# Reordering the end of the values stage of a fused decoder layer: own values before the last pages, two banks for norm sums, sample columns before variances and branch rounding

## The chip, the cores and the metric

The kernel runs on one core of one Trainium2 chip. The metric is the device time of one execution in microseconds (us), start to end, with the weights, the paged cache and the inputs in HBM. Of the kernel before there are three timed runs: 783.63, 785.12 and 786.19 us, median 785.12 us.

## The reference, cut to what matters

One inference step of a hybrid decoder layer for 256 prompt tokens and 8 sample sequences (one new token each, 1024 past tokens in pages of 128), D_MODEL 1024, all in float32:

```python
h = rms_norm(x) * (1.0 + sc2) + sh2
proj = h @ lp["w_in"]                  # q, k, v of both branches, gates g_a, g_b
o_a, o_b = attend(q_a, k_a, v_a, q_b, k_b, v_b, lam)
o_b = rms_norm(o_b, lp["subln_diff"]) * (1.0 - lam_init)
y_a = o_a.reshape(B, T, WIDTH_A) @ lp["w_branch_moba"]
y_b = o_b.reshape(B, T, WIDTH_B) @ lp["w_branch_diff"]
mixed = (jax.nn.sigmoid(g_a) * y_a + jax.nn.sigmoid(g_b) * y_b) @ lp["w_out"]
x = x + g2 * mixed
```

Before it and behind it stands a gated feed-forward block (D_FF 2816). `attend` is block-sparse attention (branch A, 8 heads of 64) and differential attention (branch B, 4 heads with values of 128); sample tokens read past keys and values through a page table. The lines above are the stretch that the change touches: the last of `attend`, the norm of `o_b`, and the two branch products.

## The kernel before, in words

Activations lie transposed: 128 features on the partitions, 264 columns (256 prompt tokens, then the 8 sample tokens) along the free axis. There are eight feature chunks c of 128; chunks 0 to 3 are branch A, 4 to 7 branch B. Every float32 weight product is made of three matmuls of rounded parts: ScalarE makes the high part of a weight block (`hi`, tile whi, line 671), VectorE or GpSimd the rest (`lo`, tile wlo, line 969 on VectorE, line 626 on GpSimd), and TensorE multiplies high by high, high by low and low by high (lines 1433 to 1435). Weight blocks have numbers; W_BR to W_BR + 3 are the four halves of the two branch matrices, W_OUT follows. whi and wlo have two buffers each, taken in turn.

The order of the work is written out by hand, engine by engine; semaphores join the engines, and each engine runs its own list strictly in that order. In the **values stage** TensorE goes through c = 0 to 7. For each c it multiplies two halves of a sequence's value pages with padded weights (line 1789, tiles kvA and kvB, three slots each, `_lent` is the third), for c = 3 and c = 7 adds the new tokens' own values (line 1803, `dcur` by `vtoks`), turns the prompt probabilities (line 1815), sums squares of a chunk of branch B over the partitions (`o_sum`, line 1772, bank 7), multiplies the prompt values (lines 1837 and 1838), and for c = 3 and c = 7 extracts the sample outputs from the masked accumulators (line 1845, 16 records of 4 columns). VectorE masks those accumulators (`om`, line 1340), takes each sum to a reciprocal variance (`o_variance`, lines 1305 and 1306), makes the low part of the branch A output (`hlo`, line 1353) and copies the extracted sample columns into qT (line 1356). ScalarE rounds these sample columns (line 925), squares those of branch B (line 926), then takes the sigmoid of all gates (line 929, after a table load), then the square root of the reciprocal variances (line 693, after another table load). VectorE scales the branch B output by it (line 1367), ScalarE rounds it (line 932), VectorE takes its low part (line 1370).

The **branch products** are four: q = 0, 1 with branch A's output into banks 0 to 3 and 4 to 7, then q = 2, 3 with branch B's output into the same banks. Each is 48 matmuls. q = 2 waits for branch B's low part (`s_olo`), for its weights, and for `s_turned_g`: VectorE must have multiplied q = 0's result by the gates (line 1378) before its banks are written again. On VectorE that instruction stands behind the low part of branch B (line 1370) and the two halves of `lo(W_BR + 2)` (line 969).

GpSimd issues the DMAs of branch B's pages in this stage (line 443), then four loads of the last conditioning weights (last_ada, line 643). SyncE issues branch A's pages and all weight blocks; a weight block's load waits until `lo` of the block that held its slot is done.

Of the kernel before, what the change touches and what calls it, by code (L numbers as in the profile page):

```python
# [25 lines left out]
KC = D // P  # L26
# [181 lines left out]
def build(nc, A, O):  # L208
    ctx = ExitStack()
    with ctx:  # L210
# [145 lines left out]
        s_pv, s_pvd, s_om, s_ext = sem("v_used"), sem("sample_out"), sem("sample_masked"), sem("sample_extracted")  # L356
# [120 lines left out]
        POOL_HALVES = 20  # L477

# [108 lines left out]
        def _(pool):  # L587
# [41 lines left out]
            for use in range(KVS, 4 * TS):  # L629
                kv_load(pool, 1, use)  # L630
                if use + 2 < POOL_HALVES:
                    lo(*filler(use + 2))
                if use in K_ROWS:
                    i = K_ROWS[use]
                    pool.wait_ge(s_tok, 4 * (i + 1))
                    row_out("k", i // 2, i % 2, ktok, ktoks, s_krow)
                if use in V_ROWS:
                    i = V_ROWS[use]
                    pool.wait_ge(s_vtok, 4 * (i + 1))
                    row_out("v", i // 2, i % 2, vtok, vtoks, s_vrow)  # L640

# [14 lines left out]
        def _(a):  # L656
# [233 lines left out]
            for c in range(KC):  # L890
# [28 lines left out]
                if c in EXTRA:  # L919
                    for t in range(2):  # L920
                        hi(EXTRA[c], t)
# [4 lines left out]
            nc.scalar.activation(osq[:, :, TP:T], qT[:, 4:8, TP:T], ACT.Square).then_inc(s_osq, 1)  # L926
            a.wait_ge(s_sig, 14)
# [31 lines left out]
        def _(v):  # L959
# [353 lines left out]
            for c in range(KC):  # L1313
                for h in range(2):
# [15 lines left out]
                    ins.then_inc(s_pscale, 1)  # L1330
                if c % 4 == 3:

                    v.wait_ge(s_pvd, c // 4 + 1)
# [15 lines left out]
                if c >= 5:  # L1349
                    o_variance(osq[:, c - 5, 0:TP], bank[:, 7, 0:TP], c - 4)  # L1350
# [9 lines left out]
            for t in range(2):  # L1360
                lo(W_BR + 1, t)
            v.wait_ge(s_pout, KC)

            o_variance(osq[:, 3, 0:TP], bank[:, 7, 0:TP], 4)
            o_variance(osq[:, :, TP:T], bank[:, 7, TP:TP + 32].rearrange("p (c s) -> p c s", s=TS), 5)
# [5 lines left out]

            for q in range(2):
# [52 lines left out]
        def _(pe):  # L1425
# [350 lines left out]
            for c in range(KC):  # L1776
# [6 lines left out]
                for half in range(2):  # L1783
                    pe.wait_ge(s_wpad, 2 * c + half + 1)
                    for ab in range(2):
                        use = 16 + 2 * c + half
                        pe.wait_ge(s_kv[ab][use % KVS], kv_landed(use))
                        for q in range(4):
                            ins = mm(bank[32 * q:32 * q + 32, 4 + ab, :], wpad[half][:, q, ab, w0:w0 + 32], kv_slot(ab, use)[:, q, :],  # L1789
                                     start=(half == 0 and c % 4 == 0), stop=(half == 1 and q > 0 and c % 4 == 3))  # L1790
# [7 lines left out]
                if c == 3:  # L1798
                    pe.wait_ge(s_dcur, 1)
                if c % 4 == 3:  # L1800
                    for ab in range(2):
                        r0 = 64 * ab + 32 * (c // 4)
                        ins = mm(bank[0:32, 4 + ab, :], dcur[:, r0:r0 + 32], vtoks[:, 512 * ab:512 * ab + 512], start=False, stop=True)
                    ins.then_inc(s_pvd, 1)
# [16 lines left out]
                if gated:  # L1821
                    gate_half(c + 1, 1)
                pe.wait_ge(s_pps, npp)
                if c:
                    pe.wait_ge(s_pout, c)
                if c >= 5:
                    o_sum(c - 1)
# [22 lines left out]
            for q in range(4):  # L1850
# [7 lines left out]
                for t in range(2):  # L1858
                    block_half(4 * half, n, n % 2, t, hhi, hlo, nk=4, w=512, k0=4 * ab)
                    if q == 0 and t == 0:  # L1860

                        pe.wait_ge(s_osq, 1)
                        pe.wait_ge(s_ovar, 4)
                        mm(bank[:, 7, TP:TP + 32].rearrange("p (c s) -> p c s", s=TS), C("ones"), osq[:, :, TP:T],
# [60 lines left out]
```

## Time and profile before

| | us |
|---|---|
| median of three runs | 785.12 |
| the profiled execution | 784.88 |
| its span, first to last instruction | 783.2 |
| outside the span | 1.68 |
| TensorE busy | 730.3 (93%) |
| VectorE busy | 479.3 (61%) |
| ScalarE busy | 320.3 (41%) |
| GpSimd busy | 123.8 (16%) |

The chain of work that ended last is 70% TensorE and 18% VectorE. The values stage lies between 417 and 522 us of the span, the branch products between 522 and 549 us. Busy shares say little here: what counts is, at each point where TensorE pauses, which engine's list it waits for. So the rows further down are mostly timelines: start, duration, engine, line, and in brackets how long the engine had been idle and what ended that. An idle time put down to "issue" has no releaser that the profile shows. TensorE's granted clock is in the rows of the view by stretch: 1.00 is 2.4 GHz, 0.50 is 1.2 GHz.

### The profile page before, as it was taken

Reading aid. Unit: us, or ns where it says so; the run is one execution under the profiler, and the core shown is the slowest. Engines: PE = TensorE matmul, PEld = TensorE weight load, DVE = VectorE, ACT = ScalarE, POOL = GpSimd, SP = SyncE. Lnnn points to the kernel's source line nnn. Section 1 sums busy time; section 2 is a strip of 40 time slices with the busy share of each in tenths; the row PEclk is TensorE's granted clock in tenths of the full one; section 3 lists DMA queues with packets and bytes.
Section 4 is the critical chain, followed back from the end, with each engine's and each line's share of the span. In section 5 each row is a group of like instructions: output and inputs, shape, how many; then the busy total and the mean of one; then the engine's idle time right before and its main releaser. Section 6 shows DMA issues by size and latency. Waiting matters only on the chain.

```text
span 783.2 us, 16961 instructions
## 1 busy us (share of the span) xinstructions
PE 730.3 (93%) x6610; PEld 647.7 (83%) x6610; DVE 479.3 (61%) x684; ACT 320.3 (41%) x515; POOL 123.8 (16%) x179
## 2 busy tenths in 40 slices
PE   5589999999999998988878999999989999999997
PEld 2369889999999797877765666669979999999997
DVE  1635454555454899999987554677766465454551
ACT  1434333344242653333314544364445444444331
POOL 0000000002000402877863332210000000000000
PEclk9799999999999999999978999999999999999999
DMA  9979898867986764999999999995625655646530
GB/s 352 381 254 344 291 321 302 269 195 267 395 277 210 273 213 142 388 400 407 405 391 342 404 403 348 342 364 191 199 72 164 205 168 171 204 148 201 165 105 28
DMA packets 116520, 209.53 MB, mean 268 GB/s; under 512 B 6714, under 2 KB 100186, under 8 KB 104162
## 3 DMA queue, kind: packets, MB, share of 16 engines
q1 hardware_dynamic: 106784, 159.47, 59.1%
q0 software_dynamic: 9440, 49.02, 16.0%
q8 instruction: 46, 0.75, 0.4%
q14 instruction: 24, 0.20, 0.1%
q10 hardware_dynamic: 226, 0.10, 0.1%
HBM read 205.31 MB, written 3.24 MB: 266 GB/s over the span
## 4 chain that ended last, share of the span: by engine, by line
PE 70%; DVE 18%; DMA 6%; issue 2%; ACT 2%; SPq 1%; ACTq 0%; DVEq 0%
PE bank L1433 19%; PE bank L1434 19%; PE bank L1435 19%; DMA early<-in_w_ada 3%; PE bank L1789 3%; DVE kvB L1152 2%; DVE kvA L1152 2%; PE bank L1484 2%; DMA kvA<-in_cache_k_moba 2%; DVE rstd L1132 2%; PE bank L1749 1%; DVE wlo L969 1%; DMA raw<-in_w_ada 1%; DVE kvB_lent L1152 1%; PE bank L1750 1%
## 5 line engine op out<-in xcount | busy, mean ns | idle before, releaser
L969 DVE TENSOR_TENSOR wlo<-raw,whi 128x1024 fp32r<-128x1024 f32 (+1 forms) x177 | 208.6, 1199 | 190.3 <-ACT whi L671 187.6
L1433 PE MATMUL bank<-hhi,whi 128*128 128x264 f32 x992 | 288.6, 291 | 11.4 <-DVE wlo L969 7.5
L1434 PE MATMUL bank<-hlo,whi 128*128 128x264 f32 x992 | 283.5, 286 | 0.0
L1435 PE MATMUL bank<-hhi,wlo 128*128 128x264 f32 x992 | 283.1, 285 | 0.0
L671 ACT ACTIVATE whi<-raw 128x1024 fp32r<-128x1024 f32 (+1 forms) x192 | 194.5, 1034 | 119.6 <-PE bank L1435 83.1
L1433 PEld LDWEIGHTS bank<-hhi,whi 128*128 128x128 f32 x992 | 189.3, 191 | 24.6 <-issue 15.1
L1434 PEld LDWEIGHTS bank<-hlo,whi 128*128 128x128 f32 x992 | 189.3, 191 | 0.2
L1435 PEld LDWEIGHTS bank<-hhi,wlo 128*128 128x128 f32 x992 | 188.4, 190 | 0.0
L1433 PE MATMUL bank<-ahi,whi 128*128 128x264 f32 x416 | 119.6, 288 | 0.4 <-DVE alo L1391 0.4
L1435 PE MATMUL bank<-ahi,wlo 128*128 128x264 f32 x416 | 118.1, 284 | 0.0
L1434 PE MATMUL bank<-alo,whi 128*128 128x264 f32 x416 | 117.8, 283 | 0.0
L1433 PEld LDWEIGHTS bank<-ahi,whi 128*128 128x128 f32 x416 | 78.2, 188 | 0.9 <-DVE alo L1391 0.6
L1434 PEld LDWEIGHTS bank<-alo,whi 128*128 128x128 f32 x416 | 78.3, 188 | 0.2
L1435 PEld LDWEIGHTS bank<-ahi,wlo 128*128 128x128 f32 x416 | 78.3, 188 | 0.0
L443 POOL DMA_DIRECT2D kvB<-in_cache_k_diff x44 | 23.2, 528 | 112.1 <-issue 64.8
L706 ACT ACTIVATE sil<-bank 128x528 f32<-128x528 f32 x22 | 13.4, 611 | 62.9 <-PE bank L1435 62.9
L710 ACT ACTIVATE ahi<-act 128x528 f32 (+1 forms) x22 | 14.2, 646 | 54.2 <-DVE act L1023 54.2
L626 POOL TENSOR_TENSOR wlo<-raw,whi 128x1024 fp32r<-128x1024 f32 x15 | 35.9, 2392 | 2.8 <-issue 2.5
L443 POOL DMA_DIRECT2D kvB<-in_cache_v_diff x44 | 23.2, 528 | 51.0 <-PE bank L1789 41.9
L1749 PE MATMUL bank<-hhi,whi 128*128 128x264 f32 x96 | 28.5, 297 | 0.0
L1027 DVE TENSOR_TENSOR alo<-act,ahi 128x528 f32 (+1 forms) x22 | 15.6, 709 | 19.1 <-ACT ahi L710 19.1
L1750 PE MATMUL bank<-hlo,whi 128*128 128x264 f32 x96 | 27.3, 284 | 0.0
(246 smaller groups left out, 804.9 us busy)
## 6 DMA issues: line engine op xcount, KB each, us to landing
raw<-in_ffn_w_gate SPq DMA_DIRECT2D x22, 1024.0 KB, 5.4
raw<-in_ffn_w_up SPq DMA_DIRECT2D x22, 1024.0 KB, 5.4
raw<-in_w_ada SPq DMA_DIRECT2D x20, 1024.0 KB, 8.3
raw<-in_w_in SPq DMA_DIRECT2D x20, 1024.0 KB, 10.5
raw<-in_ffn_w_down SPq DMA_DIRECT2D x16, 1024.0 KB, 5.3
kvB<-in_cache_k_diff POOLq DMA_DIRECT2D x44, 256.0 KB, 6.4
kvA<-in_cache_k_moba SPq DMA_DIRECT2D x44, 256.0 KB, 8.0
kvA<-in_cache_v_moba SPq DMA_DIRECT2D x44, 256.0 KB, 6.3
```

Of the source, the lines that this page charges most:

```text
L443: eng.dma_start(rows_, cache[bass.ds(page, 1)].rearrange("a (j t) d -> (a j) (t d)", t=4)).then_inc(s_kv[ab][use % KVS], 16)
L626: nc.gpsimd.tensor_tensor(half_view(wlo[n % 2], key, t), half_view(raw[s], key, t), half_view(whi[n % 2], key, t).bitcast(F32), ALU.subtra ...
L671: nc.scalar.activation(half_view(whi[key[1] % 2], key, t), half_view(raw[s], key, t), ACT.Copy).then_inc(s_hi, 1)
L969: dve.tensor_tensor(half_view(wlo[key[1] % 2], key, t), half_view(raw[s], key, t), half_view(whi[key[1] % 2], key, t).bitcast(F32), ALU.su ...
L1132: dve.reciprocal(rstd[:, i % 2, :], rstd[:, i % 2, :]).then_inc(s_krecip, 1)
L1152: dve.transpose(slot, slot).then_inc(s_kT[ab], 1)
L1433: mm(out, wh, xh, start=start, stop=False)
L1434: mm(out, wh, xl, start=False, stop=False)
L1435: return mm(out, wl, xh, start=False, stop=stop)
L1749: mm(out, wh, hhi[:, k, :], start=(k == 0), stop=False)
L1750: mm(out, wh, hlo[:, k, :], start=False, stop=False)
L1789: ins = mm(bank[32 * q:32 * q + 32, 4 + ab, :], wpad[half][:, q, ab, w0:w0 + 32], kv_slot(ab, use)[:, q, :], start=(half == 0 and c % 4 == ...
```

## The change

1. The own values of the new tokens (c = 3 and c = 7) are multiplied before the second half's pages instead of behind them, and the masking waits for the last page product. The semaphore s_pvd goes.
2. The sum of squares of c = 6 goes to bank 6, those of 4, 5 and 7 stay in bank 7, the sample columns' sum goes to bank 6. The sums wait for fewer variances.
3. On VectorE the variance of chunk 5 moves before the masking of c = 7; that of chunk 6 moves behind the sample columns; `lo(W_BR + 1)` moves to GpSimd, ahead of its last four loads.
4. On ScalarE the rounding of the sample columns and their squares move ahead of the two halves of `hi(W_BR + 1)`.

```diff
@@ gpsimd, ahead of load_last
+            for t in range(2):
+                lo(W_BR + 1, t)
@@ scalar
-                if c in EXTRA:
+                if c in EXTRA and c < KC - 1:
                     for t in range(2):
                         hi(EXTRA[c], t)
...
             nc.scalar.activation(osq[:, :, TP:T], qT[:, 4:8, TP:T], ACT.Square).then_inc(s_osq, 1)
+            for t in range(2):
+                hi(EXTRA[KC - 1], t)
             a.wait_ge(s_sig, 14)
@@ vector
+                if c == KC - 1:
+                    o_variance(osq[:, 1, 0:TP], bank[:, sum_bank(5), 0:TP], 2)
                 if c % 4 == 3:
-                    v.wait_ge(s_pvd, c // 4 + 1)
+                    v.wait_ge(s_pv, 16 * (c // 4 + 1))
...
-                if c >= 5:
-                    o_variance(osq[:, c - 5, 0:TP], bank[:, 7, 0:TP], c - 4)
+                if c == 5:
+                    o_variance(osq[:, 0, 0:TP], bank[:, sum_bank(4), 0:TP], 1)
...
-            for t in range(2):
-                lo(W_BR + 1, t)
+            o_variance(osq[:, 2, 0:TP], bank[:, sum_bank(6), 0:TP], 3)
             v.wait_ge(s_pout, KC)
...
+            v.wait_ge(s_lo, half_done(W_BR + 1, 1))
             for q in range(2):
                 for t in range(2):
                     lo(W_BR + 2 + q, t)
@@ tensor
+                    if half and c % 4 == 3:
+                        pe.wait_ge(s_dcur, 1)
+                        for ab in range(2):
+                            r0 = 64 * ab + 32 * (c // 4)
+                            mm(bank[0:32, 4 + ab, :], dcur[:, r0:r0 + 32], vtoks[:, 512 * ab:512 * ab + 512], start=False, stop=False)
                     pe.wait_ge(s_wpad, 2 * c + half + 1)
...
-                if c > 4:
-                    pe.wait_ge(s_ovar, c - 4)
-                mm(bank[:, 7, 0:TP], C("ones"), osq[:, c - 4, 0:TP], start=True, stop=True).then_inc(s_osum, 1)
+                if c in (5, 7):
+                    pe.wait_ge(s_ovar, (c - 3) // 2)
+                mm(bank[:, sum_bank(c), 0:TP], C("ones"), osq[:, c - 4, 0:TP], start=True, stop=True).then_inc(s_osum, 1)
```

How the instructions of ScalarE stand at the end of the stage, from the last pair that handles chunk 7 on. Before (whi_55 from raw_51 is `hi(W_BR + 1)`, gT the gates, osq the squares and later the reciprocal roots):

```order
L917 ACTIVATE osq<-bank 128x256
L671 ACTIVATE whi_55<-raw_51 128x4x256 x2
L925 ACTIVATE hhi<-qT 128x4x8
L926 ACTIVATE osq<-qT 128x4x8
L929 ACT_TABLE_LOAD
L929 ACTIVATE gT<-gT 128x1056 x4
L693 ACT_TABLE_LOAD
L693 ACTIVATE osq<-osq 128x1056
```

The same place now, with the changed kernel's line numbers:

```order
L925 ACTIVATE osq<-bank 128x256
L933 ACTIVATE hhi<-qT 128x4x8
L934 ACTIVATE osq<-qT 128x4x8
L679 ACTIVATE whi_55<-raw_51 128x4x256 x2
L939 ACT_TABLE_LOAD
L939 ACTIVATE gT<-gT 128x1056 x4
L701 ACT_TABLE_LOAD
L701 ACTIVATE osq<-osq 128x1056
```

The two roundings of the weights have moved from ahead of the sample columns to between them and the sigmoids.

VectorE at the same place, before, from the masking on (hlo<-qT 128x4x256 is the low part of branch A, the copy of 128x8x4 brings the sample columns):

```order
L1340 TENSOR_TENSOR om<-bank,const 128x512 x2
L1305 TENSOR_SCALAR osq<-bank 128x256
L1306 RECIPROCAL osq<-osq 128x256
L1353 TENSOR_TENSOR hlo<-qT,hhi 128x4x256
L1356 COPY qT<-bank 128x8x4
L1359 TENSOR_TENSOR hlo<-qT,hhi 128x4x8
L969 TENSOR_TENSOR wlo_57<-raw_51,whi_55 128x4x256 x2
L1305 TENSOR_SCALAR osq<-bank 128x256
L1306 RECIPROCAL osq<-osq 128x256
L1305 TENSOR_SCALAR osq<-bank 128x4x8
L1306 RECIPROCAL osq<-osq 128x4x8
L1367 SCALAR_TENSOR_TENSOR qT<-qT,misc,osq 128x1056
```

And now:

```order
L1352 TENSOR_TENSOR om<-bank,const 128x512 x2
L1365 TENSOR_TENSOR hlo<-qT,hhi 128x4x256
L1368 COPY qT<-bank 128x8x4
L1371 TENSOR_TENSOR hlo<-qT,hhi 128x4x8
L1315 TENSOR_SCALAR osq<-bank 128x256
L1316 RECIPROCAL osq<-osq 128x256
L1315 TENSOR_SCALAR osq<-bank 128x256
L1316 RECIPROCAL osq<-osq 128x256
L1315 TENSOR_SCALAR osq<-bank 128x4x8
L1316 RECIPROCAL osq<-osq 128x4x8
L1378 SCALAR_TENSOR_TENSOR qT<-qT,misc,osq 128x1056
```

The variance of chunk 6 stands behind the sample columns instead of ahead of the low part, and the two subtractions into wlo_57 are gone from this list.

They stand in GpSimd's list, behind its last page loads and ahead of its last four weight loads:

```order
L443 DMA kvB_96<-in_cache_v_diff 32x2048
L631 TENSOR_TENSOR wlo_57<-raw_51,whi_55 128x4x256 x2
L651 DMA last_ada_131<-in_w_ada 128x2x1024
L651 DMA last_ada_132<-in_w_ada 128x2x1024
L651 DMA last_ada_133<-in_w_ada 128x2x1024
L651 DMA last_ada_134<-in_w_ada 128x2x1024
```

So the four loads wait behind them, and they behind ScalarE's roundings.

## Rows read from the trace of the kernel before

**Rows 1.** Timeline of TensorE: start us, us, engine, line, operation [idle before <-releaser].
```profile
514.80 1.90 PE L1803 MATMUL bank<-vtoks,dcur 8*32 8x512 f32 x4
...
518.95 1.85 PE L1845 MATMUL bank<-const,om 128*128 128x4 f32 x16
...
522.42 0.39 PE L1433 MATMUL bank<-hhi,whi 128*128 128x264 f32 x1 [0.90 <-DVE hlo L1359]
...
535.80 0.28 PE L1435 MATMUL bank<-hhi,wlo 128*128 128x264 f32 x1
537.29 0.36 PE L1433 MATMUL bank<-hhi,whi 128*128 128x264 f32 x1 [1.21 <-issue]
```

**Rows 2.** Timeline of VectorE, end of the values stage and branch products.
```profile
516.74 1.29 DVE L1340 TENSOR_TENSOR om<-bank,const 128x512 f32<-128x512 f32 x2 [2.11 <-PE bank L1803]
518.50 0.42 DVE L1305 TENSOR_SCALAR osq<-bank 128x256 f32<-128x256 f32 x1 [0.47 <-PE bank L1772]
...
520.63 1.16 DVE L1353 TENSOR_TENSOR hlo<-qT,hhi 128x1024 fp32r<-128x1024 f32 x1
521.70 0.18 DVE L1356 COPY qT<-bank 128x32 f32<-128x32 f32 x1
...
522.29 2.35 DVE L969 TENSOR_TENSOR wlo<-raw,whi 128x1024 fp32r<-128x1024 f32 x2
...
527.55 0.35 DVE L1306 RECIPROCAL osq<-osq 128x32 f32<-128x32 f32 x1
530.02 1.32 DVE L1367 SCALAR_TENSOR_TENSOR qT<-qT,misc,osq 128x1056 f32<-128x1056 f32 x1 [2.12 <-ACT osq L693]
532.49 1.26 DVE L1370 TENSOR_TENSOR hlo<-qT,hhi 128x1056 fp32r<-128x1056 f32 x1 [1.15 <-ACT hhi L932]
533.67 2.35 DVE L969 TENSOR_TENSOR wlo<-raw,whi 128x1024 fp32r<-128x1024 f32 x2
535.94 1.25 DVE L1378 TENSOR_TENSOR gT<-bank,gT 128x1056 f32<-128x1056 f32 x1
```

**Rows 3.** Timeline of ScalarE, the same stretch.
```profile
519.69 2.00 ACT L671 ACTIVATE whi<-raw 128x1024 fp32r<-128x1024 f32 x2
521.92 0.23 ACT L925 ACTIVATE hhi<-qT 128x32 fp32r<-128x32 f32 x1 [0.22 <-DVE qT L1356]
...
522.28 1.28 ACT L929 ACT_TABLE_LOAD   x1
523.58 4.01 ACT L929 ACTIVATE gT<-gT 128x1056 f32<-128x1056 f32 x4
527.60 1.28 ACT L693 ACT_TABLE_LOAD   x1
528.90 1.09 ACT L693 ACTIVATE osq<-osq 128x1056 f32<-128x1056 f32 x1
531.37 1.09 ACT L932 ACTIVATE hhi<-qT 128x1056 fp32r<-128x1056 f32 x1 [1.38 <-DVE qT L1367]
```

**Rows 4.** Line 626, all GpSimd subtractions: ns min/median/max, first and last start.
```profile
L626 POOL TENSOR_TENSOR wlo<-raw,whi x15: 2368/2395/2403, 310.0 to 403.8; 128x1024 fp32r<-128x1024 f32 x15
```

**Rows 5.** Timeline, a page slot's reload behind c = 3, and its use.
```profile
463.97 2.46 SPq L443 DMA_DIRECT2D kvA_lent<-in_cache_v_moba  x4
...
485.31 1.06 PE L1789 MATMUL bank<-kvA_lent,wpad 128*32 128x512 f32 x8
```

**Rows 6.** Timeline of TensorE, three starts after pauses.
```profile
423.34 0.38 PE L1693 MATMUL bank<-sm,const 128*128 128x2 f32 x2 [2.06 <-ACT ncur L806]
425.09 1.56 PE L1815 MATMUL bank<-const,plog 128*128 128x128 f32 x6 [1.37 <-DVE plog L1329]
...
583.26 0.36 PE L1433 MATMUL bank<-hhi,whi 128*128 128x264 f32 x1 [1.49 <-DVE hlo L1016]
```

**Rows 7.** View by stretch: PE, PEld, DVE, ACT, POOL busy, PEclk, DMA share, GB/s.
```profile
424.00:425.00 1.00, 0.00 (x0) 0.00 (x0) 0.96 (x5) 0.00 (x0) 0.00 (x0) 0.50 1.07 369
...
522.00:528.00 6.00, 5.58 (x33) 5.58 (x34) 5.09 (x7) 5.95 (x8) 0.52 (x1) 0.72 0.98 370
```

More of the change, by code:

```diff
@@ L355, in build @@
         s_pT, s_pTs = sem("probs_turned"), sem("probs_turned_ready")
-        s_pv, s_pvd, s_om, s_ext = sem("v_used"), sem("sample_out"), sem("sample_masked"), sem("sample_extracted")
+        s_pv, s_om, s_ext = sem("v_used"), sem("sample_masked"), sem("sample_extracted")
         s_psc, s_plog, s_pexp, s_pscale = sem("prompt_scores"), sem("prompt_logits"), sem("prompt_exp"), sem("prompt_probs")
@@ L477, in build, with sum_bank @@
         POOL_HALVES = 20
+        def sum_bank(c):
+            return 6 if c == 6 else 7
         AHEAD = {4: [W_KV + 5], 6: [W_KV + 6], 8: [W_KV + 7], 10: [W_GATE], 12: [W_GATE + 1], 14: [W_GATE + 2],
@@ L1359, in _ @@
             dve.tensor_tensor(hlo[:, 0:4, TP:T], qT[:, 0:4, TP:T], hhi[:, 0:4, TP:T].bitcast(F32), ALU.subtract).then_inc(s_olo, 1)
-            for t in range(2):
-                lo(W_BR + 1, t)
+            o_variance(osq[:, 2, 0:TP], bank[:, sum_bank(6), 0:TP], 3)
             v.wait_ge(s_pout, KC)
-            o_variance(osq[:, 3, 0:TP], bank[:, 7, 0:TP], 4)
-            o_variance(osq[:, :, TP:T], bank[:, 7, TP:TP + 32].rearrange("p (c s) -> p c s", s=TS), 5)
+            o_variance(osq[:, 3, 0:TP], bank[:, sum_bank(7), 0:TP], 4)
+            o_variance(osq[:, :, TP:T], bank[:, 6, TP:TP + 32].rearrange("p (c s) -> p c s", s=TS), 5)
             v.wait_ge(s_orstd, 1)
@@ L1789, in _ @@
                             ins = mm(bank[32 * q:32 * q + 32, 4 + ab, :], wpad[half][:, q, ab, w0:w0 + 32], kv_slot(ab, use)[:, q, :],
-                                     start=(half == 0 and c % 4 == 0), stop=(half == 1 and q > 0 and c % 4 == 3))
+                                     start=(half == 0 and c % 4 == 0), stop=(half == 1 and c % 4 == 3))
                         ins.then_inc(s_pv, 1)
@@ L1797, in _ @@
                     exp_sums(1)
[L1798 to L1804, printed above, removed]
                 for h in range(2 if c < 4 else 1):
@@ L1822, in _ @@
                     gate_half(c + 1, 1)
+                if 5 <= c < KC - 1:
+                    o_sum(c - 1)
                 pe.wait_ge(s_pps, npp)
+                if c == KC - 1:
+                    o_sum(c - 1)
                 if c:
                     pe.wait_ge(s_pout, c)
-                if c >= 5:
-                    o_sum(c - 1)
                 if c == 2:
@@ L1862, in _ @@
                         pe.wait_ge(s_osq, 1)
-                        pe.wait_ge(s_ovar, 4)
-                        mm(bank[:, 7, TP:TP + 32].rearrange("p (c s) -> p c s", s=TS), C("ones"), osq[:, :, TP:T],
+                        pe.wait_ge(s_ovar, 3)
+                        mm(bank[:, 6, TP:TP + 32].rearrange("p (c s) -> p c s", s=TS), C("ones"), osq[:, :, TP:T],
                            start=True, stop=True).then_inc(s_osum, 1)
```

## The prediction, made before the changed kernel was run

> **What bounds the kernel now.** I read the page first: one core, TensorE busy 93% of the span, so a change pays only where TensorE pauses, and costs where it makes TensorE pause longer. Then I read TensorE's timeline around the diff for bracketed idle times. There are two that the change can move. At 522.42 the first branch product starts after 0.90 us of idle; the releaser is hlo, the low part of the sample columns. At 537.29 the third branch product starts after 1.21 us of idle, which the view puts down to "issue" [rows 1]. The second has to be explained by hand, because "issue" only means that no releaser is shown. The code lists three conditions for q = 2, and VectorE's timeline dates them: branch B's low part ends at 532.49 + 1.26 = 533.75, the first half of the weights' low part about 534.9, and the gating of q = 0's result ends at 535.94 + 1.25 = 537.19, 0.10 us before the product starts [rows 1, 2]. So TensorE waits for VectorE's gating, not for its own queue.
>
> Now the chain behind that gating, backward through rows 2 and 3. The gating (535.94) stands right behind two subtractions (533.67), these right behind hlo (532.49), which waited 1.15 us for ScalarE's rounding (531.37), which waited for VectorE's scaling (530.02), which had been idle 2.12 us until ScalarE's root (528.90 + 1.09 = 529.99). On ScalarE nothing is idle before the root: table load 527.60, four sigmoids 523.58, table load 522.28, squares and rounding of the sample columns 521.92, and these waited for VectorE's copy of the sample columns (521.70) [rows 2, 3]. The root's other condition, the last variance, was ready at 527.55 + 0.35 = 527.90, 1.00 us before the root began [rows 2, 3]. So from 521.70 to 537.29 the path is: sample columns, ScalarE's list, VectorE's list, third product. TensorE's first two products (522.42 to 536.08) lie beside it with 1.21 us to spare.
>
> **The change part by part.**
>
> *Own values before the last pages.* It is the same four records, 1.90 us, in either place, and TensorE did not pause before any page product there [rows 1]; the masking still follows the last of them. At c = 7: 0. At c = 3 a page slot comes free 1.8 us later. Its reload went out at 463.97 and its use began at 485.31, so 21.3 us shrink to 19.5 [rows 5]; the four transfers took 2.46 us to issue. 0. Were the reload to take more than 19.5 us, the price would be the excess, at most 1.8.
>
> *Variances and banks.* VectorE's list after the masking (516.74 + 1.29 = 518.03) was: variance of chunk 6 from 518.50, low part of branch A from 520.63, copy from 521.70. The variance takes 520.63 - 518.50 = 2.13 us, plus 0.47 of waiting for its sum [rows 2]. Without it the low part (1.16) ends at about 519.2, and the copy waits for TensorE's extraction instead, 518.95 + 1.85 = 520.80 [rows 1]. Between a shown end and the start it releases there are 0.04 us (copy 521.88, rounding 521.92 [rows 2, 3]). So the copy goes from 521.70 to 520.84: 0.86 us earlier, and with it the start of the first branch product, 522.42 to 521.56. The variance of chunk 5 moves into VectorE's 2.11 us of idle before the masking [rows 2]: it needs 2.13, its place begins that much earlier because the same instructions stood before the probabilities: 0. The variance of chunk 6 now starts about 521.55, that of 7 ends about 525.9, and the sample sum's variance follows TensorE's half product at about 526.1 plus 0.9: 527.0. That is ahead of the root and still not its last condition.
>
> *Low part of W_BR + 1 on GpSimd.* On VectorE it was 2.35 us from 522.29 [rows 2], beside ScalarE's sigmoids and on no path. GpSimd needs 2.37 to 2.40 us for each half [rows 4]. ScalarE's high parts will be there at about 522.5 and 523.4, so GpSimd works from 522.6 to 525.0 and on to 527.4. TensorE wants the first half at q = 1, which follows 48 matmuls: before, q = 0 and q = 1 together took 522.42 to 536.08, so q = 1 starts near 529, at the earliest (with a full clock) 527.5 for the first half and 530.4 for the second. Cover 2.5 us; if the subtractions took twice as long, the second half would be ready at 532.1 and TensorE would pause 1.7 us, which the later pause absorbs. 0. Queued behind them on GpSimd are the four last_ada loads, issued from 527.4 on, wanted only behind the output product. SyncE's load for slot raw_51 moves from about 524.7 to 527.4; its rounding comes last in the output product. 0.
>
> *ScalarE's list.* This is the step that counts. Before, the two halves of hi(W_BR + 1) ran 519.69 to 521.69 in the gap in which ScalarE had to wait for the sample columns anyway [rows 3]: they cost nothing there. Now ScalarE waits idle until 520.88, does the two small instructions (0.36 us before the table load, as 521.92 to 522.28), and then 2.00 us of rounding before the sigmoid's table load. Table load: 522.28 - 0.86 + 2.00 = 523.42, that is **+1.14 us**. Everything behind it on the path is unchanged in size: root, scaling, rounding, low part, two subtractions, gating. The third product starts at 537.29 + 1.14 = 538.43. TensorE, meanwhile, is 0.86 us early with its second product: pause 1.21 + 0.86 + 1.14 = **3.21 us** instead of 1.21. Bounds of this term: the pitch of two roundings could be read as 1.95 to 2.06, the 0.86 as 0.7 to 0.9, so +1.05 to +1.35. After 537.29 TensorE works without a long pause to 553, so a late start is passed on whole.
>
> *The clock in the longer pause.* The trace has no pause of 3.2 us here, so this is bounded. After 1.49 us of idle at 583.26 the next product's first matmul took 0.36 us, the full-clock size. After 2.06 us, two small matmuls and 1.37 us more, the clock stood at 1.2 GHz [rows 6, 7]. It also fell behind own values, extraction and the 0.90 pause: the mean over 522 to 528 is 0.72, and 0.28 of 6 us lost at a loss of half is 3.4 us at 1.2 GHz [rows 7]. Such a stretch over dense matmuls costs half its length: 1.7 us at most; if it begins inside the pause, part of it falls on idle time. Bounds 0 and 1.7; 3.21 is nearest to the case with 2.06 and 1.37, where it fell, so I take **1.2 us**.
>
> The Trainium skill ("TensorE: Matmul & The Clock Gate", "What's actually happening") says that the slow clock is the default and only activity lifts it, and under "HAM oscillation — how this bites in real kernels" that waits between bursts of matmuls cost the clock each time. By that rule the pause that this change lengthens is paid for twice; the rows above bear it out for the larger pause and not for the 1.49 one. Without the rule the sum below would be the same.
>
> Sum, against the profiled execution: 784.88 + 1.14 + 1.2 = 787.2 us. Its span is 783.2, so 1.68 lie outside and do not change. The median of the three runs is 0.24 above that execution; I leave this in the range.
>
> **The rivals.**
>
> *Late root, clock stays up.* 784.88 + 1.14 = 786.0 us. For it: at 583.26 and at 537.29 itself the clock held through 1.49 and 1.21 us. Against it: 3.21 is longer than any pause here that the clock survived.
>
> *The first product's start is what counts (faster).* If "issue" at 537.29 were TensorE's own delay and not the gating, the end would follow the first product: 0.86 us earlier, 784.0. If in addition the shorter pause before it kept the clock at 2.4 GHz, where before 3.4 us ran at half, another 1.7: 782.3. It decides from the point at which the third product starts less than 0.35 us behind the second. For it: the view names no releaser. Against it: the gating's end and the start agree to 0.10 us, and the code has that wait.
>
> *GpSimd's subtractions are late.* They would have to end after 538.4 less half a product, some 8 us beyond plan, to cost anything; each further us costs one. About 789. For it: nothing in the 15 samples, which spread by 0.04 us [rows 4].
>
> *Nothing moves.* ScalarE's 2.00 us and the 0.86 could cancel further if the extraction ended earlier; 785.0. It would need 1.1 us more than the rows give.
>
> **How the numbers follow.** Late root with a fallen clock 0.48 (786.4 to 788.0); late root with full clock 0.32 (785.3 to 786.7); first product counts 0.10 (half of it with the clock's gain); nothing moves 0.07; GpSimd late 0.03. The likeliest gives 787.2. A measurement of this kernel tells changes from about 0.3%, 2.36 us, on: below 782.8 and above 787.5. Above 787.5 lies some 0.55 of the first case and the last: 0.30. Below 782.8 lie half of the third and a little scatter: 0.07. The rest, 0.63, is no change that can be told. For 8 in 10 the range runs from 784.0, leaving out the clock's gain, to 788.6, where the first case meets the runs' upper scatter.
>
> **What would show it.** VectorE's copy of the sample columns at about 520.8 and the first product at 521.6; ScalarE's two roundings between the squares and the sigmoid's table load, which begins at 523.4; root at 530.0 to 531.1; the third product at 538.4 after a pause of over 3 us (over 4 if the first product ran at full clock); granted clock 0.50 in some stretch between 536 and 543. GpSimd's subtractions end by 527.5. I am wrong if the root is not later than before, if the third product starts without a long pause, or if the time falls.

## Result: 0.4% slower, and the profile after

| | before | changed |
|---|---|---|
| median, 14 runs each | 786.06 us | 788.64 us |
| ratio, 95% interval | | 1.0037 (1.0020 to 1.0055) |
| profiled execution | 784.88 us | 789.50 us |
| its span | 783.2 us | 787.8 us |
| TensorE busy | 730.3 us | 733.4 us |

The change costs 0.37% by the ratio and 2.58 us by the two medians. One of the 14 executions before took 2558.71 us; without it that median is 785.92. The forecast's direction and its path were right; the time lies 0.04 us above the upper end of the range. Two sizes are behind that: in the profiled execution the clock in the longer pause cost about twice what I took, and with more runs the median of the kernel before itself rose by 0.94 us over the three runs shown.

All times inside the spans are compared from one common point, the start of the extraction of the sample columns (TensorE, 16 matmuls of 128x4): 518.95 in the trace before [rows 1], 520.20 here. From one profile to another of the kernels below this point lies anywhere from 518.28 to 522.50. Most of that (3.6 us) has arisen before the values stage begins; and even from the stage's first page product to this point two kernels that are the same up to here ("changed" and "changed, pause filled" below) took 101.86 and 102.28 us. So spans and single executions can't be compared to 1 us, but distances from this point can. Behind the start of the second feed-forward block's first product all traces agree (199.9 us to the end). Between the two points the kernel before takes 64.31 us and the changed one 67.71: **+3.40 us**.

TensorE after (start us, us, engine, line, operation, idle before with its releaser), against [rows 1]:

```profile
514.20 1.90 PE L1800 MATMUL bank<-vtoks,dcur 8*32 8x512 f32 x4
...
520.20 1.85 PE L1857 MATMUL bank<-const,om 128*128 128x4 f32 x16
...
522.82 0.39 PE L1445 MATMUL bank<-hhi,whi 128*128 128x264 f32 x1 [0.24 <-DVE hlo L1371]
...
534.64 0.28 PE L1447 MATMUL bank<-hhi,wlo 128*128 128x264 f32 x1
539.59 0.56 PE L1445 MATMUL bank<-hhi,whi 128*128 128x264 f32 x1 [4.67 <-DVE gT L1390]
```

The first product starts 2.62 us behind the extraction's start instead of 3.47. The third starts 19.39 behind it instead of 18.34, after a pause of 4.67 us instead of 1.21, and this time the view names VectorE's gating, which had to be found by hand before.

ScalarE after, against [rows 3]:

```profile
522.31 0.23 ACT L933 ACTIVATE hhi<-qT 128x32 fp32r<-128x32 f32 x1 [1.25 <-DVE qT L1368]
522.45 0.21 ACT L934 ACTIVATE osq<-qT 128x32 f32<-128x32 f32 x1
522.57 2.00 ACT L679 ACTIVATE whi<-raw 128x1024 fp32r<-128x1024 f32 x2
524.58 1.28 ACT L939 ACT_TABLE_LOAD   x1
525.88 4.01 ACT L939 ACTIVATE gT<-gT 128x1056 f32<-128x1056 f32 x4
529.90 1.28 ACT L701 ACT_TABLE_LOAD   x1
531.20 1.09 ACT L701 ACTIVATE osq<-osq 128x1056 f32<-128x1056 f32 x1
533.67 1.09 ACT L942 ACTIVATE hhi<-qT 128x1056 fp32r<-128x1056 f32 x1 [1.39 <-DVE qT L1378]
```

VectorE after, against [rows 2]:

```profile
519.23 1.21 DVE L1365 TENSOR_TENSOR hlo<-qT,hhi 128x1024 fp32r<-128x1024 f32 x1
522.09 0.19 DVE L1368 COPY qT<-bank 128x32 f32<-128x32 f32 x1 [1.65 <-PE bank L1857]
522.58 0.19 DVE L1371 TENSOR_TENSOR hlo<-qT,hhi 128x32 fp32r<-128x32 f32 x1 [0.30 <-ACT hhi L933]
...
527.03 0.35 DVE L1316 RECIPROCAL osq<-osq 128x32 f32<-128x32 f32 x1
532.32 1.32 DVE L1378 SCALAR_TENSOR_TENSOR qT<-qT,misc,osq 128x1056 f32<-128x1056 f32 x1 [4.93 <-ACT osq L701]
534.79 1.26 DVE L1381 TENSOR_TENSOR hlo<-qT,hhi 128x1056 fp32r<-128x1056 f32 x1 [1.15 <-ACT hhi L942]
535.97 2.35 DVE L979 TENSOR_TENSOR wlo<-raw,whi 128x1024 fp32r<-128x1024 f32 x2
538.24 1.25 DVE L1390 TENSOR_TENSOR gT<-bank,gT 128x1056 f32<-128x1056 f32 x1
```

On ScalarE nothing is idle from 522.31 to the root's end. The two roundings (2.00 us) stand between the squares and the sigmoid's table load, and the root starts 11.00 us behind the extraction's start instead of 9.95. VectorE has finished its variances at 527.38 and then waits 4.93 us for it (before: 2.12).

TensorE's granted clock by stretch (PE, PEld, DVE, ACT, POOL busy, PEclk, DMA share, GB/s), against the 0.72 of 522:528 in [rows 7]:

```profile
522.00:528.00 6.00, 5.76 (x46) 5.36 (x46) 4.90 (x8) 5.66 (x8) 4.08 (x2) 1.00 0.00 0
...
537.50:541.00 3.50, 1.41 (x6) 1.44 (x7) 3.50 (x4) 1.04 (x2) 0.00 (x0) 0.57 1.03 412
541.00:545.00 4.00, 4.00 (x21) 4.00 (x20) 1.92 (x2) 0.00 (x0) 0.00 (x0) 0.52 1.03 381
545.00:551.00 6.00, 6.00 (x51) 6.00 (x50) 4.32 (x6) 2.88 (x4) 0.00 (x0) 1.00 0.79 252
```

The stretch at 1.2 GHz (0.5) over the first product is gone, and a longer one has come over the third: from about 538.0, inside the pause, to 544.8. Compare the matmul counts: 21 in 4 us at the low clock against 51 in 6 at the full one.

### The profile page after: what moved, and what is told of

Its sections match the earlier page's. It is cut to its first block, busy times and chain, and to the rows that moved or that the text cites. A ratio compares the mean times of both kernels' runs of the same rounds, so it can differ in the third digit from the quotient of the medians.

```text
span 787.8 us, 16960 instructions
## 1 busy us (share of the span) xinstructions
PE 733.4 (93%) x6610; PEld 651.4 (83%) x6610; DVE 477.9 (61%) x682; ACT 320.1 (41%) x515; POOL 128.5 (16%) x181
## 4 chain that ended last, share of the span: by engine, by line
PE 70%; DVE 17%; DMA 6%; ACT 3%; issue 2%; SPq 1%; ACTq 0%; DVEq 0%
PE bank L1445 19%; PE bank L1446 18%; PE bank L1447 18%; DMA early<-in_w_ada 3%; PE bank L1806 3%; DVE kvA L1162 2%; DVE kvB L1162 2%; PE bank L1496 2%; DMA kvA_lent<-in_cache_k_moba 2%; PE bank L1761 1%; DVE wlo L979 1%; DVE kvA_lent L1162 1%; DVE kvB_lent L1162 1%; PE bank L1762 1%; PE bank L1763 1%
## 5 line engine op out<-in xcount | busy, mean ns | idle before, releaser
L979 DVE TENSOR_TENSOR wlo<-raw,whi 128x1024 fp32r<-128x1024 f32 (+1 forms) x175 | 206.3, 1199 | 189.6 <-ACT whi L679 186.7
L631 POOL TENSOR_TENSOR wlo<-raw,whi 128x1024 fp32r<-128x1024 f32 x17 | 40.6, 2391 | 23.7 <-issue 23.1
```

Source lines behind the costliest of these rows:

```text
L631: nc.gpsimd.tensor_tensor(half_view(wlo[n % 2], key, t), half_view(raw[s], key, t), half_view(whi[n % 2], key, t).bitcast(F32), ALU.subtra ...
L979: dve.tensor_tensor(half_view(wlo[key[1] % 2], key, t), half_view(raw[s], key, t), half_view(whi[key[1] % 2], key, t).bitcast(F32), ALU.su ...
```

## Experiments

Names: "X" is the extraction's start. "Start 1", "root", "start 3" and "to block 2" are the distances from X to the first branch product, the root, the third branch product and the second feed-forward block. Each distance comes from one profiled execution, each ratio from five rounds of runs in turn with the kernel before; "GpSimd made to wait" was executed only once (785.37 us). The theory: the end follows ScalarE's list to the root, and the pause before the third product pulls the clock down. The rival: the moves ahead of the first product, or the contention of GpSimd with VectorE, cost the time.

| kernel | start 1 | root | pause, start 3 | to block 2 | ratio (95%) |
|---|---|---|---|---|---|
| before | 3.47 | 9.95 | 1.21, 18.34 | 64.31 | 1 |
| changed | 2.62 | 11.00 | 4.67, 19.39 | 67.71 | 1.0037 (1.0020–1.0055) |
| roundings back ahead | 4.39 | 9.64 | 0.23, 18.03 | 64.00 | 1.0003 (0.9976–1.0030) |
| only roundings behind | 3.48 | 11.85 | 2.06, 20.24 | 67.74 | 1.0057 (1.0034–1.0081) |
| changed, pause filled | 2.62 | 10.99 | 1.54, 19.39 | 65.35 | 1.0025 (1.0002–1.0047) |
| root ahead of sigmoids | 4.39 | 11.11 | 2.52, 20.43 | 67.97 | 1.0048 (1.0029–1.0068) |
| only own values | 3.47 | 9.94 | 1.20, 18.33 | 64.30 | 1.0000 (0.9982–1.0019) |
| only GpSimd's low part | 5.13 | 11.70 | 0.23, 20.09 | 66.07 | 1.0024 (1.0005–1.0044) |
| low part on VectorE | 3.15 | 9.62 | 1.23, 18.01 | 63.97 | 0.9997 (0.9979–1.0016) |
| GpSimd made to wait | 3.14 | 9.61 | 1.23, 18.00 | 63.97 | one execution |
| gates early | 2.62 | 7.22 | 1.85, 16.57 | 64.05 | 0.9996 (0.9977–1.0015) |
| gates early, low part split | 2.62 | 7.22 | 0.89, 15.62 | 61.58 | **0.9961 (0.9943–0.9978)** |
| the same, pause filled | 2.62 | 7.22 | none shown | 61.59 | 0.9987 (0.9968–1.0006) |

**Undo the rounding alone.** The changed kernel, with the two roundings of W_BR + 1 ahead of the sample columns again; everything else stays changed.

```diff
-                if c in EXTRA and c < KC - 1:
+                if c in EXTRA:
...
-            for t in range(2):
-                hi(EXTRA[KC - 1], t)
```

> The changed kernel with one edit undone: ScalarE's two roundings of W_BR + 1 stand again ahead of the sample columns. Theory (late root): the root comes 2.0 us earlier than in the changed kernel, the third branch product with it, its pause falls from 4.67 to about 2.7 us, and the clock costs less or nothing: 2.0 to 4.3 us below the changed kernel, that is 0 to 1.7 us below the kernel before (ratio 0.998 to 1.000). Rival (the other edits cost the time: own values, banks, subtractions on GpSimd): the time stays near the changed kernel's, ratio about 1.003.

Measured 64.00 us to block 2 and a ratio of 1.0003: the whole loss is gone, the root is 0.31 us earlier than before the change, and the clock stays up over the third product. The root came 1.36 us earlier than in the changed kernel, not 2.0: the copy of the sample columns is over at 520.98 here, but ScalarE is still at the two roundings and takes the columns only at 521.54. Ahead of the earlier columns the roundings are no longer free. And the first product came late, at 4.39 us, so the pause before the third shrank to 0.23 instead of 2.7. GpSimd and VectorE in this kernel:

```profile
520.85 2.34 POOL L631 TENSOR_TENSOR wlo<-raw,whi 128x1024 fp32r<-128x1024 f32 x1 [18.55 <-issue]
...
521.80 1.43 DVE L1369 TENSOR_TENSOR hlo<-qT,hhi 128x32 fp32r<-128x32 f32 x1 [0.82 <-ACT hhi L933]
```

VectorE's 32-column subtraction takes 1.43 us instead of 0.19 and ends at 523.23; GpSimd's ends at 523.19. It was held until GpSimd was done. In the changed kernel this can't happen: GpSimd's input comes after the roundings, at 523.75, when the short subtraction is over.

**Do the rounding alone.** The kernel before with only these two lines moved behind the squares (the reverse of the diff above).

> The kernel before with only ScalarE's part of the change: the two roundings of W_BR + 1 between the sample columns' squares and the sigmoids. Theory: the first product starts as before, table load for the sigmoids, root and third product come 2.0 us later, the pause before the third product grows from 1.21 to about 3.2 us, and where the clock falls in it another 1 to 2.3 us: ratio 1.0025 to 1.0055. Rival (the other edits cost the time): ratio within 1.001.

The time is lost in full: +3.43 us to block 2, 1.90 of it by the root and 1.53 by the clock. The ratio, 1.0057, is some 4.5 us; its lower end, 1.0034, is 2.7. The root is later than in the full change since the copy of the sample columns is not earlier here. TensorE's start and the stretch behind it:

```profile
538.52 0.36 PE L1435 MATMUL bank<-hhi,whi 128*128 128x264 f32 x1 [2.06 <-issue]
```
```profile
539.00:542.90 3.90, 3.90 (x22) 3.90 (x21) 2.85 (x3) 0.00 (x0) 0.00 (x0) 0.56 0.92 309
```

**Fill the pause.** The changed kernel with 28 matmuls of 240 columns into a part of a bank that nobody reads, ahead of the second half of q = 1: they take TensorE's time that was idle, and nothing waits longer.

```diff
+                    if q == 1 and t == 1:
+                        for f in range(28):
+                            mm(bank[:, 7, T:T + 240], hhi[:, f % 4, 0:P], hhi[:, f % 4, 0:240], start=True, stop=True)
```

> The changed kernel with 28 matmuls of 240 columns more (their results are not used) between the two halves of the second branch product, so that TensorE works through most of the pause. Theory (late root 1.0 to 1.1 us plus a fallen clock of up to 2.3 us): the third product starts as late as in the changed kernel, but at 2.4 GHz, and the time falls by 1 to 2.3 us against the changed kernel, ratio to the kernel before about 1.0015. Rival (the clock costs nothing, only the wait counts): time as the changed kernel, 1.0035.

This divides the loss, as far as one profiled execution of each kernel can. Start 3 is where it was (19.39), the pause is 1.54 us, the clock stays at 1.00, and the way to block 2 is 65.35 us:

```profile
534.13 3.29 PE L1873 MATMUL bank<-hhi 128*128 128x240 f32 x28
```
```profile
543.00:547.00 4.00, 4.00 (x35) 4.00 (x34) 3.52 (x4) 0.00 (x0) 0.00 (x0) 1.00 1.03 389
```

35 matmuls in 4 us, against 21 above. So 67.71 - 65.35 = 2.36 us were the clock, and 65.35 - 64.31 = 1.04 the late root. The ratio, 1.0025, agrees with +1.04 us (1.0013) within its interval and is no sharper than that; by ratios alone this kernel can't be told from the changed one.

**The root ahead of the sigmoids.** The changed kernel with the roundings back ahead, and in the list behind the squares: root, rounding of branch B, then the sigmoids between the later roundings.

```diff
-            for q in range(4):
-                nc.scalar.activation(gT[:, 4 * q:4 * q + 4, :], gT[:, 4 * q:4 * q + 4, :], ACT.Sigmoid).then_inc(s_sigend, 1)
             root(osq[:, :, :], s_ovar, 5, s_orstd)
...
+            hi(W_BR + 2, 0)
+            hi(W_BR + 2, 1)
+            for q in range(3):
+                gates(q)
...
```

> e1 with the root of the norm taken ahead of the gates' sigmoids on ScalarE; the sigmoids stand behind the weights' rounding for the third product. Theory (the chain from the sample columns over ScalarE's list to the gating sets the third product): the root comes right behind the last variance, some 3 us earlier, the gating at about 534 us, TensorE then waits for itself: the third product starts at the end of the second, with a pause under 0.5 us. Against e1 1.0 to 2.7 us faster, ratio to the kernel before 0.995 to 0.998. Rival (something else holds the third product): no gain over e1.

A miss: 1.0048. ScalarE shows why:

```profile
531.97 1.28 ACT L701 ACT_TABLE_LOAD   x1 [6.83 <-DVE osq L1323]
533.26 1.09 ACT L701 ACTIVATE osq<-osq 128x1056 f32<-128x1056 f32 x1
...
538.74 1.28 ACT L939 ACT_TABLE_LOAD   x1
540.03 3.03 ACT L939 ACTIVATE gT<-gT 128x1056 f32<-128x1056 f32 x3
```

With the sigmoids gone from in front of it, the root waits for its other condition, the last variance, which hangs on TensorE's half product, and the root's table load waits with it instead of being done before (6.83 us idle, then 1.28 of load). The gating then waits for the sigmoids. What the list had been hiding was another chain: the last variance was ready 8.95 us behind X in the kernel before, where the root began at 9.95. Here it is ready only at 9.73, since this kernel, too, has its first product at 4.39 and at the low clock; so the miss is in part the same late first product, and no run has this order without it.

**The other parts, each alone.** Own values ahead of the second half's pages in the kernel before (and the masking on the page products' count); and GpSimd's low part in the kernel before.

```diff
+                    if half and c % 4 == 3:
+                        pe.wait_ge(s_dcur, 1)
...
-                    v.wait_ge(s_pvd, c // 4 + 1)
+                    v.wait_ge(s_pv, 16 * (c // 4 + 1))
...
```

> The kernel before with only the own values moved ahead of the second half's pages and the mask waiting for the last page product. Theory: no instruction on the path changes its place: first product 3.5, root 9.95, third product 18.3 us behind the extraction's start, as before; ratio 0.999 to 1.001. Rival (the page slot that comes free 1.8 us later delays a load that is waited for): a pause before a page product between 480 and 500 us, ratio 1.001 to 1.003.

No distance moves by more than 0.01 us. The change itself lies ahead of X, where these distances don't reach; there TensorE has no pause before a page product between 480 and 500 us, and the ratio leaves room for 1.5 us either way.

```diff
+            for t in range(2):
+                lo(W_BR + 1, t)
+
             def load_last(e):
...
```

> The kernel before with only this part of the change: the two subtractions for W_BR + 1 on GpSimd instead of VectorE. Theory (engines with two inputs in SBUF hold each other up): GpSimd's first subtraction waits for VectorE's low part of branch A and then holds VectorE's low part of the sample columns, so that the first product starts about 5.3 us behind the extraction's start instead of 3.5; the root is not touched, TensorE's own two products then bound the third: about 19 us instead of 18.3, ratio 1.000 to 1.002. Rival (no such hold): first product at 3.5, ratio 1.000.

The first product came late as expected; that the root would not move was wrong, it came 1.75 us later. Three rows, VectorE, GpSimd, VectorE (one timeline):

```profile
520.62 1.16 DVE L1356 TENSOR_TENSOR hlo<-qT,hhi 128x1024 fp32r<-128x1024 f32 x1
520.89 3.09 POOL L626 TENSOR_TENSOR wlo<-raw,whi 128x1024 fp32r<-128x1024 f32 x1 [18.42 <-issue]
...
522.17 1.85 DVE L1362 TENSOR_TENSOR hlo<-qT,hhi 128x32 fp32r<-128x32 f32 x1 [0.30 <-ACT hhi L928]
```

Each holds the other in turn: GpSimd's takes 3.09 us instead of 2.38 behind VectorE's, then VectorE's 1.85 instead of 0.19 behind GpSimd's. The first product starts after 2.56 us of idle, runs at 1.2 GHz until 529.9, and the half product behind it, on which the last variance hangs, is late. The root's releaser confirms it:

```profile
530.65 1.09 ACT L696 ACTIVATE osq<-osq 128x1056 f32<-128x1056 f32 x1 [1.77 <-DVE osq L1309]
```

**Contention or order.** Two kernels from the one with the roundings back ahead. In one the low part of W_BR + 1 goes back to VectorE, ahead of its wait for the root; in the other it stays on GpSimd but waits for the sample columns' low part.

```diff
-            for t in range(2):
-                lo(W_BR + 1, t)        # GpSimd
...
+            for t in range(2):
+                lo(W_BR + 1, t)        # VectorE
             v.wait_ge(s_orstd, 1)
...
```

> e1 with the two subtractions for W_BR + 1 back on VectorE, behind the last variance, and none on GpSimd. Theory (GpSimd's subtraction, which began at 520.85 in e1, held VectorE's low part of the sample columns for its whole length: 1.43 us instead of 0.19): that instruction takes 0.19 us again and the first product starts 3.1 us behind the extraction's start instead of 4.4; the third product as in e1 or up to 0.3 us earlier, at about 18.0 behind it. Ratio to the kernel before 0.998 to 1.000. Rival (the 1.43 us have another cause): the instruction stays above 1 us.

```diff
+            pool.wait_ge(s_olo, 1)
             for t in range(2):
                 lo(W_BR + 1, t)
```

> e1 with GpSimd's two subtractions made to wait until VectorE has finished the low part of the sample columns. Nothing else moves. Theory (the two engines hold each other up): VectorE's instruction takes 0.19 us, the first product starts 3.1 us behind the extraction's start, GpSimd's subtractions take 2.4 us each from then on. Rival: it stays at 1.4 us.

Both bring start 1 from 4.39 to 3.15 us and leave the rest (63.97). In the second:

```profile
522.65 0.19 DVE L1370 TENSOR_TENSOR hlo<-qT,hhi 128x32 fp32r<-128x32 f32 x1 [0.82 <-ACT hhi L934]
...
522.94 2.38 POOL L631 TENSOR_TENSOR wlo<-raw,whi 128x1024 fp32r<-128x1024 f32 x1 [19.78 <-DVE hlo L1370]
```

Both operations have their undisturbed length again, on the same engines. The 1.24 us were the overlap, and the end didn't care: the pause before start 3 took them up (0.23 against 1.23).

**Shorten the list.** From the kernel with the low part on VectorE: sigmoids 0 to 2 and their table load move into ScalarE's 4.4 us of idle ahead of the last probabilities, before X, one rounding goes behind the squares, and a one-element root ahead of the real one brings its table load forward.

```diff
+                    a.wait_ge(s_sig, 14)
+                    for q in range(3):
+                        gates(q)
...
-                    for t in range(2):
+                    for t in range(1 if c == KC - 1 else 2):
...
+            hi(EXTRA[KC - 1], 1)
+            gates(3)
+            nc.scalar.activation(misc[:, 20:21], misc[:, 21:22], ACT.Sqrt)
```

> f1 with three of the four sigmoids of the gates in ScalarE's 4.3 us of idle ahead of the last probabilities, the fourth and the second rounding of W_BR + 1 behind the sample columns, and the root's table load ahead of the root's wait. Theory (ScalarE's list between the sample columns and the root is what sets the third product): the root begins with the last variance, about 8.3 us behind the extraction's start instead of 9.95, and the third product is then bound by TensorE's own second product, 16.3 to 16.8 us behind it against 18.3 in the kernel before: 1.6 to 2 us less, ratio 0.997 to 0.999. Rival (the gating chain has another bound): third product no earlier than 17.5.

The root came at 7.22 us and start 3 at 16.57, 1.77 us earlier than before; yet block 2 only 0.26 earlier, and the time is the same. TensorE and its clock:

```profile
537.42 0.36 PE L1447 MATMUL bank<-hhi,whi 128*128 128x264 f32 x1 [1.85 <-issue]
```
```profile
538.00:542.00 4.00, 4.00 (x23) 4.00 (x22) 2.75 (x3) 0.00 (x0) 0.00 (x0) 0.57 0.95 309
```

A pause of 1.85 us cost 1.5 us behind it. The first matmul behind the pause still had its full-clock 0.36 us; the clock fell at about 538.4, inside the product. And the pause was still VectorE's, not TensorE's own second product as expected: the root ended at 529.16, and the scaling began only at 530.16, when VectorE was through with both halves of the low part. So the next kernel shortens the pause, too: one half of the low part goes behind VectorE's scaling, beside ScalarE's rounding, where VectorE waited anyway.

```diff
-            for t in range(2):
-                lo(W_BR + 1, t)
+            lo(W_BR + 1, 0)
             v.wait_ge(s_orstd, 1)
...
+            lo(W_BR + 1, 1)
             v.wait_ge(s_ohi, 3)
```

> f3 with the second half of W_BR + 1's low part moved behind VectorE's scaling by the root. Theory: in f3 the scaling started 1.0 us behind the root's end, since VectorE was busy; now it starts with it, and the third product starts 15.6 us behind the extraction's start where the first product runs at full clock (16.3 where it does not), against 18.34 in the kernel before; the pause is 1 us or less and the clock stays up. From the extraction to the first product of the second feed-forward block: 61.6 to 62.3 us against 64.31. Ratio 0.9965 to 0.9985. Rival (the clock falls anyway, as in f3): 63.1 to 64, ratio 0.999.

0.9961, outside the interval of no change, 782.51 us against 785.12: this version beats both kernels. Its ScalarE, VectorE and TensorE (three views):

```profile
525.81 1.07 ACT L885 ACTIVATE gT<-gT 128x1056 f32<-128x1056 f32 x1
526.90 1.28 ACT L940 ACT_TABLE_LOAD   x1
528.20 0.20 ACT L940 ACTIVATE misc<-misc 128x1 f32<-128x1 f32 x1
529.72 1.09 ACT L698 ACTIVATE osq<-osq 128x1056 f32<-128x1056 f32 x1 [1.32 <-DVE osq L1317]
```
```profile
530.84 1.32 DVE L1380 SCALAR_TENSOR_TENSOR qT<-qT,misc,osq 128x1056 f32<-128x1056 f32 x1
532.08 1.22 DVE L980 TENSOR_TENSOR wlo<-raw,whi 128x1024 fp32r<-128x1024 f32 x1
533.32 1.26 DVE L1384 TENSOR_TENSOR hlo<-qT,hhi 128x1056 fp32r<-128x1056 f32 x1
```
```profile
538.12 0.36 PE L1447 MATMUL bank<-hhi,whi 128*128 128x264 f32 x1 [0.89 <-issue]
```
```profile
538.00:542.00 4.00, 3.88 (x32) 3.92 (x33) 4.00 (x5) 0.38 (x1) 0.00 (x0) 1.00 0.92 297
```

The table load is over before the last variance (idle 1.32 at the root is all that is left), the pause is 0.89 us and the clock holds: 32 matmuls where the kernel before this one had 23. Of the 2.73 us, 18.34 - 15.62 = 2.72 are the earlier third product.

Last, the same with eight fill matmuls in what pause is left.

```diff
+                        for f in range(8):
+                            mm(bank[:, 7, T:T + 240], hhi[:, f % 4, 0:P], hhi[:, f % 4, 0:240], start=True, stop=True)
```

> g1 with 8 matmuls of 240 columns (results not used) between the halves of the second product, about 0.9 us. Theory: TensorE has no pause before the third product, the clock does not fall there; 61.7 to 62.3 us from extraction to the second feed-forward block where the first product runs at full clock, up to 63.2 where it does not. Ratio as g1 or 0.001 lower. Rival (the clock depends on other things than this pause): as many slow stretches as in g1.

Nothing is gained: 61.59 us to block 2, as without them. Its ratio of 0.9987 is weaker than 0.9961, and by itself can't be told from no change; the intervals overlap (0.9968 to 0.9978), the traces show no difference behind X, and why it should be slower stays open.

## Why the prediction was right and where it was wrong

*The path: right.* "From 521.70 to 537.29 the path is: sample columns, ScalarE's list, VectorE's list, third product." The chain of waits after names these pieces one by one from 522.09 to 539.59, and moving the two roundings alone brings the loss (1.0057) or takes it away (1.0003).

*Own values, 0; variances and banks, 0.86: right as far as it shows.* Own values alone leave every distance within 0.01 us; their price ahead of X is known only to 1.5 us, by the ratio. Start 1 came 0.85 us earlier in the change; variances and banks had no run of their own.

*Low part on GpSimd, 0: right in this change, by luck of the order.* Its two subtractions ran undisturbed (GpSimd after):

```profile
523.75 2.38 POOL L631 TENSOR_TENSOR wlo<-raw,whi 128x1024 fp32r<-128x1024 f32 x1 [20.16 <-issue]
526.31 2.41 POOL L631 TENSOR_TENSOR wlo<-raw,whi 128x1024 fp32r<-128x1024 f32 x1 [0.17 <-POOL wlo L631]
```

I priced them by their own length and by when TensorE wants them, and did not ask what they do to VectorE. Alone, the same move cost 1.76 us to block 2. It is the roundings behind the sample columns that keep the two apart.

*ScalarE's list, +1.14: right, 1.05 measured*, at the lower bound. The rounding of the sample columns came 2.11 us behind the extraction's start instead of 2.97, which is the 0.86 of the sum ("idle until 520.88" should have read 521.06, but the sum didn't use it). The two roundings followed it after 0.26 us, where the table load had taken 0.36 to follow, and with their 2.01 us to the table load that makes 0.26 + 2.01 - 0.36 - 0.86 = 1.05.

*The clock in the longer pause, 1.2 with a bound of 1.7: the mechanism right, the size wrong, 2.36 measured.* The failed sentence is "Such a stretch over dense matmuls costs half its length: 1.7 us at most". I had taken the longest stretch at 1.2 GHz from one mean (0.72 over 522:528, so 3.4 us), and made it the bound for every stretch. Here it lasted 6.8 us, 538.0 to 544.8, and 5.2 us of it lay over matmuls, which started 0.22 us apart instead of 0.12: 5.2 x 0.10 / 0.22 = 2.4. So the rule of half was nearly right and its length wrong. The trace before could have told: [rows 7] shows one microsecond of another stretch, and that one is twice as long as the 3.4 that I took. First before, then, at the same place, the changed kernel without and with the filled pause:

```profile
422.00:432.00 10.00, 7.30 (x48) 3.80 (x52) 8.79 (x25) 4.16 (x16) 3.92 (x7) 0.66 0.93 341
424.00:434.00 10.00, 8.61 (x73) 4.56 (x73) 7.48 (x23) 4.28 (x14) 2.77 (x6) 0.66 1.02 393
424.00:434.00 10.00, 6.74 (x64) 3.95 (x68) 9.28 (x27) 4.16 (x17) 4.43 (x8) 0.83 0.98 338
```

A mean of 0.66 over 10 us is 6.8 us at 1.2 GHz, one of 0.83 is 3.4. The last two kernels are the same up to X, so the same work met one length in one execution and half of it in another. The 2.36 us are therefore the price in the execution that was profiled (789.50, above the median of 788.64). By the ratio the change costs 2.9 us (1.6 to 4.3), which leaves 1.9 us for the clock in the usual execution, with 0.5 to 3.3 possible. My 1.2 lies inside that, so how far it was off in the median execution stays open; what failed is the bound.

The reading of the 1.49 us pause was right by luck: the clock did hold there (1.00 over 583:587), but a first matmul of 0.36 us doesn't show it. With the gates early it took 0.36, and the clock fell 1 us later.

The pause, too, was longer than in the sum: 3.21 held only if the first product ran slow. It ran at full clock, 1.6 us shorter, and since the third product waits for the chain, all of that went into the pause: 1.21 + 0.85 + 1.05 + 1.56 = 4.67. The text named this ("over 4") and gave it no price. So the earlier first product gave back nothing and made the pause longer. Whether the longer pause is why the stretch was long is not shown: the same lengths occur above behind equal work.

The Trainium skill ("TensorE: Matmul & The Clock Gate", "HAM oscillation — how this bites in real kernels") says that waits between bursts of matmuls cost the clock each time. Ahead of the third product the traces agree for the longer pauses only. The clock fell behind start 3 in the four traces with pauses of 1.85, 2.06, 2.52 and 4.67 us, and held in those with 0.23, 0.89, 1.20, 1.21, 1.23 and 1.54.

*The base.* Forecast against the profiled execution of 784.88: +2.3 us. By the traces +3.40, by the ratio 0.0037 x 786.06 = +2.9, by the medians +2.58. So of the 1.44 us between 787.2 and 788.64 the medians put only 0.26 on the change; 1.18 are the base, 786.06 instead of 784.88. A range built on a median of three runs should have carried that 1 us on its upper side.

*The rivals.* "First product counts" is out: it came 0.85 us earlier and the end later. "Late root, clock stays up" is what the filled pause shows (+1.04), so it was a size of the same path. "GpSimd late" and "nothing moves" did not occur.

## What to carry to other kernels

When instructions are moved behind a wait on an engine, their price is the idle time that they filled before: on a path, two roundings that were free cost nearly their full length. When the waiting engine is TensorE, a late release is paid for a second time by the clock once the pause is long enough (before the third product here with 1.85 us and more, not with 1.54 and less, in one trace each), and an improvement of what stands ahead of the pause only lengthens it; shorten the chain that ends the pause, then look whether what remains of it is short enough. Before an elementwise operation goes to GpSimd, look at which two-input operations of VectorE run beside it, not only at when its result is wanted.

## What the hardware showed that I had not expected

*VectorE and GpSimd hold each other.* A subtraction of VectorE with both inputs in SBUF took 1.43 and 1.85 us instead of 0.19 beside a subtraction of GpSimd, and ended within 0.05 us of it; in the other order GpSimd's took 3.09 instead of 2.38. With the two set one behind the other both were back at 0.19 and 2.38. The Trainium skill ("SBUF — State Buffer", "Who interferes with whom") says that a VectorE instruction with two SBUF inputs contends with a GpSimd instruction that reads SBUF, that the ports they share are an exclusive lock, and that the order of issue decides who blocks; these rows agree, in both orders.

*The clock behind a short pause.* Over the first product it fell in each of the eight traces with 0.76 us or more of idle before that product (0.76, 0.90, and up to 2.56), and in none of the five with 0.23 or 0.24. The same 0.89 to 1.54 us before the third product did nothing. What comes before differs: 16 matmuls of 4 columns and two of 256 ahead of the first product, two whole products of 264 columns ahead of the third. That this difference is the reason was not tested. Nor is each of these counts more than one execution per kernel, and at the start of the values stage the same work ran 3.4 us at 1.2 GHz in one execution and 6.8 in another.
